# Paged keys by an indirect DMA over 128 partitions, transposed in 32x32 blocks on VectorE, in a hybrid decoder step

## What is computed

```python
cache_k, cache_v (DEPTH, N_PHYS_PAGES, PAGE_SIZE, N_HEADS, HEAD_DIM)   # 1, 160, 128, 8, 128
page_table       (DEC_BATCH, N_PAGES) int32                            # 8, 16
idx, valid = dsa_select(iq, iw, ik_all, q_pos, topk)                   # best 256 of 2056 keys
k_sel, v_sel = rows idx of the paged cache, or of the 8 new keys
logits = einsum('bthd,btkhd->bthk', q, k_sel) * ATT_SCALE + rel_bias[rel_bucket(q_pos - idx)]
out = einsum('bthk,btkhd->bthd', softmax(where(valid, logits, -inf)), v_sel)
```

## Time and profile before

| | |
|---|---|
| median of 3 runs | 1597.6 us (1593.25 to 1598.45) |
| profiled execution | 1593.25 us, span 1593.2 us |
| mean granted TensorE clock | 0.957 |
| key stages, first to last matmul | 464.6 to 582, 705.9 to 812 us |
| value stages | 595.7 to 705.9, 828.4 to 929 us |
| bytes read from HBM | 240.28 MB |

### The profile page before, as it was taken

How to read it: one execution, slowest core, us unless ns; L and a number is a source line. 1 busy time by engine, 2 the same in 40 slices (tenths; PEclk the granted TensorE clock), 3 DMA queues, 4 the chain that set the end, 5 groups by cost and what they waited for, 6 DMA issues and landing times.

```text
span 1593.2 us, 32571 instructions
## 1 busy us (share of the span) xinstructions
PE 1471.7 (92%) x13518; PEld 1334.5 (84%) x13518; DVE 762.0 (48%) x1030; ACT 511.5 (32%) x818; POOL 234.5 (15%) x371
## 2 busy tenths in 40 slices
PE   7999998979979989899998998899799999999995
PEld 4867798957867778797777998799699999999995
DVE  5288699496514540025540135543555555552123
ACT  4243223324323341023341122122344455442121
POOL 3423234154210000000000000321000110000000
PEclk8899999989999999999999999899799999999998
DMA  5415223122159979999869976133322233223221
GB/s 173 149 27 159 65 80 113 57 96 73 49 188 369 332 249 342 383 358 329 310 223 402 363 258 240 34 125 104 113 80 80 80 90 95 83 98 102 79 83 60
DMA packets 179278, 266.58 MB, mean 167 GB/s; under 512 B 20522, under 2 KB 136539, under 8 KB 178043
## 3 DMA queue, kind: packets, MB, share of 16 engines
q1 hardware_dynamic: 167947, 243.95, 44.5%
q0 software_dynamic: 5104, 11.11, 2.1%
q10 hardware_dynamic: 6080, 9.44, 1.6%
HBM read 240.28 MB, written 24.18 MB: 166 GB/s over the span
## 4 chain that ended last, share of the span: by engine, by line
PE 77%; DVE 8%; DMA 5%; ACT 3%; SPq 2%; issue 2%; POOL 2%; ACTq 0%; DVEq 0%
PE PS L987 14%; PE PS L989 13%; PE PS L988 13%; PE PS L1197 8%; PE PS L1210 4%; PE PS L1245 3%; PE PS L1319 3%; PE PS L1318 3%; PE PS L1317 3%; DMA R<-in_cache_v 3%; PE PS L1028 2%; PE PS L1029 2%; PE PS L1030 2%; PE PS L1173 1%; PE PS L1120 1%
## 5 line engine op out<-in xcount | busy, mean ns | idle before, releaser
L987 PE MATMUL PS<-xn_hi,WH 128*128 128x288 f32 (+1 forms) x1424 | 430.7, 302 | 16.0 <-DVE xn_lo L1614 13.2
L988 PE MATMUL PS<-xn_lo,WH 128*128 128x288 f32 (+1 forms) x1424 | 424.7, 298 | 0.0
L989 PE MATMUL PS<-xn_hi,WL 128*128 128x288 f32 (+1 forms) x1424 | 424.6, 298 | 0.0
L987 PEld LDWEIGHTS PS<-xn_hi,WH 128*128 128x128 f32 (+1 forms) x1424 | 271.1, 190 | 33.1 <-issue 22.2
L988 PEld LDWEIGHTS PS<-xn_lo,WH 128*128 128x128 f32 (+1 forms) x1424 | 271.9, 191 | 0.0
L989 PEld LDWEIGHTS PS<-xn_hi,WL 128*128 128x128 f32 (+1 forms) x1424 | 271.6, 191 | 0.0
L582 DVE TENSOR_TENSOR WL<-W,WH 128x2048 fp32r<-128x2048 f32 (+2 forms) x69 | 145.7, 2112 | 241.6 <-ACT WH L1358 241.6
L1358 ACT ACTIVATE WH<-W 128x2048 fp32r<-128x2048 f32 (+2 forms) x81 | 145.1, 1791 | 90.2 <-PE PS L1319 74.9
L1197 PE MATMUL PS<-CST,R 128*128 128x128 f32 x1024 | 142.7, 283 | 9.8 <-DMA R<-in_cache_k 9.5
L1793 DVE COPY RB<-PS 128x512 f32<-128x512 f32 x128 | 88.3, 691 | 115.7 <-PE PS L1197 115.7
L1197 PEld LDWEIGHTS PS<-CST,R 128*128 128x128 f32 x1024 | 112.1, 143 | 35.9 <-issue 25.7
(11 more groups left out here) (257 smaller groups left out, 2423.2 us busy)
## 6 DMA issues: line engine op xcount, KB each, us to landing
R<-in_cache_k SPq DMA_DIRECT2D x128, 512.0 KB, 5.3
R<-in_cache_v SPq DMA_DIRECT2D x128, 512.0 KB, 7.0
W<-in_w_in SPq DMA_DIRECT2D x30, 1024.0 KB, 5.4
W<-in_w_up SPq DMA_DIRECT2D x44, 512.0 KB, 4.6
W<-in_w_down SPq DMA_DIRECT2D x16, 704.0 KB, 4.4
x_scratch<-xT SPq DMA_DIRECT2D x2, 2304.0 KB, 9.0
W<-in_w_branch_a SPq DMA_DIRECT2D x4, 1024.0 KB, 7.9
W<-in_w_branch_b SPq DMA_DIRECT2D x4, 1024.0 KB, 6.1
```

Source lines behind the costliest of these rows:

```text
L987: pe.matmul(out, hi[:, k, cols], x.hi_block(n)[:, tokens], start=first, stop=False)
L988: pe.matmul(out, hi[:, k, cols], x.lo_block(n)[:, tokens], start=False, stop=False)
L989: return pe.matmul(out, lo[:, k, cols], x.hi_block(n)[:, tokens], start=False, stop=last)
```

## The change

Keys are now loaded four pages at a time: one indirect DMA (`load_keys`), issued by GpSimd, takes 128 rows of 16 KB, each of them four successive keys of one page, 32 rows from the page of each of four requests, into 128 partitions. `KROW` holds the row numbers, worked out on GpSimd from the page table (page number x 32 + lane). Two such tiles of 2 MB take the place of the ring's eight pages. VectorE turns a tile in two halves of four heads by 32x32 block transposes into three buffers `KTB`; a block transpose leaves partition 32b+d with number d of 32 of request b's rows. TensorE multiplies these directly: for each head four products over 32 of the 128 dimensions each, with `QB`, in which the queries lie block-diagonally by request; the PE transposes, their PSUM tiles `kp` and the copies to `KTb` go. The keys then stand in the order (key mod 4, key div 4). So mask and bias are read in that order (`by_rest`), and value pages are loaded so that row 4k+r of a page lands in partition 32r+k.

`QB` is cleared by GpSimd and filled by 32 activations on ScalarE. The mask's store and its reload for the first group move from SP's queue to ScalarE's. The tiles `kl` and `o` take one single bank each in the place of a pair. Five side tiles now stand in the key stage of each group (after tiles 2, 5, 8, 11, 14), two in each softmax, one in each of the value stage's first seven requests, two at the start, one at the end. The first eight value pages of a group wait for the transposes of the last two key tiles, and the first two key tiles of the second group for value pages 60 and 64.

```diff
     side = ([('sv', c, r) for c in range(4) for r in range(R)] + [('ga', c) for c in range(8)]
             + [('gb', c) for c in range(8)] + [('su', c) for c in range(8)])
     SIDE_B = [(1, 1), (1, 1), (1, 1), (1, 1), (1, 2), (1, 2), (1, 2), (1, 2)]
-    two, three = {7: 1, 16: 1}, {4: 1, 10: 1, 16: 1}
-    SIDE_V = [two, two, two, three, two, two, three, {4: 1, 10: 1}]
+    SIDE_K = [2, 5, 8, 11, 14]
+    SIDE_V = [{8: 1}, {8: 1}, {8: 1}, {8: 1}, {8: 1}, {8: 1}, {8: 1}, {}]
     side_at, todo = {}, list(side)
 
...
     for G in range(2):
-        put_side(('softmax', G, 0), 1)
+        for kp in SIDE_K:
+            put_side(('K', G, kp), 1)
+        put_side(('softmax', G, 0), 2)
...
-        QZ = R3[:, 4352:6400].rearrange("p (h b c) -> p h b c", h=H, b=8)
+        QB = R3[:, 4352:6400].rearrange("p (g h j c) -> p g h j c", g=2, h=H, j=4)
         kTn = blocks(R3[:, 6400:7424], H)
-        KTb = [blocks(RB[:, 1024 * i:1024 * i + 1024], H) for i in range(2)]
+        KR = [blocks(R1[:, 4096 * i:4096 * i + 4096], 4) for i in range(2)]
+        KTB = [blocks(a, 4) for a in (RB[:, 0:2048], R3[:, 0:2048], R3[:, 2048:4096])]
...
-            G, kind, n = (seq - 8) // 128, (seq - 8) // 64 % 2, (seq - 8) % 64
-            if kind == 0:
-                e.wait_ge(single_filled, single.slots['kp', G, n, 1][0] + 1)
+            G, kind, n = seq // 128, seq // 64 % 2, seq % 64
+            if kind == 0 and n >= 8:
+                e.wait_ge(S_("k_transposed"), 32 * G + 2 * (n // 4 - 1))
+            elif kind == 0:
+                e.wait_ge(S_("v_pages_used"), 64 * G - 4 + 4 * (n // 4))
+            elif n < 8:
+                e.wait_ge(S_("k_transposed"), 32 * G + 30 + 2 * (n // 4))
             else:
-                e.wait_ge(S_("v_pages_used"), 64 * G + n + 1)
+                e.wait_ge(S_("v_pages_used"), 64 * G + n - 7)
...
+        def load_page(e, seq):
+
+            if seq >= 256:
+                return
+            G, kind, n = seq // 128, seq // 64 % 2, seq % 64
+            page_freed(e, seq)
+            v = page_id(e, 4 * G + n // 16, n % 16)
+            e.dma_start(ring[seq % 8], cache_v[0, bass.ds(v, 1)].rearrange("o (k r) h d -> (o r) k (h d)", r=4))\
+                .then_inc(page_in[seq % 8], 16)
+
+        def load_keys(e, G, kp):
+
+            page_freed(e, 128 * G + 4 * kp)
+            e.indirect_dma_start(out=R1[:, 4096 * (kp % 2):4096 * (kp % 2) + 4096], out_offset=None,
+                                 in_=cache_k[0].rearrange("n (k r) h d -> (n k) (r h d)", r=4),
+                                 in_offset=bass.IndirectOffsetOnAxis(ap=KROW[:, 16 * G + kp:16 * G + kp + 1], axis=0))\
+                .then_inc(key_in[kp % 2], 16)
...
             side_loads('start')
-            for seq in range(4):
-                load_page(seq)
-
-            sp.wait_ge(S_("sample_mask"), 1)
-            sp.dma_start(mask_scr, S).then_inc(S_("mask_out"), 16)
-            sp.wait_ge(S_("mask_out"), 16)
-            for j in range(4):
-                sp.dma_start(MG[32 * j:32 * j + 32, :], mask_scr[0:32, :]).then_inc(S_("mask_in0"), 16)
-            for seq in range(4, 8):
-                load_page(seq)
+
             for G in range(2):
-                for n in range(64):
-                    load_page(128 * G + n + 8)
+                for kp in range(NPAGES):
+                    side_loads('K', G, kp)
+                for n in range(8):
+                    load_page(sp, 128 * G + 64 + n)
                 side_loads('softmax', G, 0)
                 side_loads('softmax', G, 1)
                 for b in range(4):
                     for kp in range(NPG):
                         if kp < NPAGES:
-                            load_page(128 * G + 64 + 16 * b + kp + 8)
+                            if 16 * b + kp + 8 < 64:
+                                load_page(sp, 128 * G + 64 + 16 * b + kp + 8)
                         side_loads('V', G, b, kp)
...
+            pool.wait_ge(S_("rows_in"), 64)
+            pool.wait_ge(S_("consts_in"), 16)
+            link(pool.tensor_copy(RB[:, 32:64], PROW[:, :]))
+            link(pool.tensor_scalar(RB[:, 32:64], RB[:, 32:64], 32.0, const('lane')[:, 0:1], ALU.mult, ALU.add))
+            link(pool.tensor_copy(KROW[:, :], RB[:, 32:64]))
...
+            pool.memset(QB, 0.0).then_inc(S_("queries_cleared"), 1)
+            load_keys(pool, 0, 0)
...
-                for n in range(65):
-                    if n < 64:
-                        seq = 128 * G + n
-                        pe.wait_ge(page_in[seq % 8], 16 * (seq // 8 + 1))
-                        for u in range(2):
-                            claim(pe, 'kp', G, n, u)
-                            for i in range(4):
-                                h = 4 * u + i
-                                last = pe.transpose(bank('kp', G, n, u)[:, P * i:P * i + P],
-                                                    ring[seq % 8][:, HD * h:HD * h + HD], ident)
-                            done(last, 'kp', G, n, u)
-                    if (G, n) == (0, 1):
+                for kp in range(NPAGES):
+                    if (G, kp) == (0, 0):
                         pe.wait_ge(S_("sample_queries"), 1)
-                    if n:
-                        kp, bb = (n - 1) // 4, (n - 1) % 4
-                        if bb == 0:
-                            claim(pe, 'kl', G, kp)
-                        for u in range(2):
-                            drained(pe, 'kp', G, n - 1, u)
-                            for j in range(4):
-                                h = 4 * u + j
-                                last = pe.matmul(pbank('kl', G, kp)[32 * j:32 * j + 32, u, 0:P],
-                                                 QZ[:, h, 4 * G + bb, :], KTb[(n - 1) % 2][:, h, :],
-                                                 start=(bb == 0), stop=(bb == 3))
-                        if bb == 3:
+                    claim(pe, 'kl', G, kp)
+                    for u in range(2):
+                        pe.wait_ge(S_("k_transposed"), 32 * G + 2 * kp + u + 1)
+                        keys = KTB[(2 * kp + u) % 3]
+                        for j in range(4):
+                            for c in range(4):
+                                last = pe.matmul(bank('kl', G, kp)[32 * c:32 * c + 32, P * u:P * u + P],
+                                                 QB[:, G, 4 * u + c, j, :],
+                                                 keys[:, :, P * c + 32 * j:P * c + 32 * j + 32],
+                                                 start=(j == 0), stop=(j == 3))
+                        if u == 0:
+                            last.then_inc(S_("k_half_used"), 1)
+                        else:
                             done(last, 'kl', G, kp)
+                    sides('K', G, kp)
...
-                for n in range(64):
-                    filled(dve, 'kp', G, n, 1)
-                    dve.tensor_copy(KTb[n % 2][:, 4:8, :], blocks(bank('kp', G, n, 1), 4))\
-                        .then_inc(drains('kp', G, n, 1), 1)
-                    if n % 4 == 0 and n:
-                        logits(n // 4 - 1)
-                    if n == 48:
+                def transposed(kp):
+
+                    dve.wait_ge(key_in[kp % 2], 16 * (8 * G + kp // 2 + 1))
+                    for u in range(2):
+                        n = 2 * kp + u
+                        if n in (1, 2):
+                            if G == 0:
+                                filled(dve, 'pv', H - 1)
+                            else:
+                                filled(dve, 'o', 0, 3)
+                        if n >= 3:
+                            if n % 2 == 0:
+                                filled(dve, 'kl', G, (n - 3) // 2)
+                            else:
+                                dve.wait_ge(S_("k_half_used"), 16 * G + (n - 3) // 2 + 1)
+                        elif G and n == 0:
+                            filled(dve, 'kl', 0, NPAGES - 1)
+                        dve.transpose(KTB[n % 3], KR[kp % 2][:, :, 512 * u:512 * u + 512])\
+                            .then_inc(S_("k_transposed"), 1)
+
+                for kp in range(NPAGES):
+                    transposed(kp)
+                    if kp >= 2:
+                        logits(kp - 2)
+                    if kp == 13:
                         drained(dve, 'kl', G, 11)
                         dve.tensor_reduce(EARLY, LS[:, :, 0:12 * P], AX_X, ALU.max)
+                    splits('K', G, kp)
...
+def by_rest(a):
+
+    return a.rearrange("p (k r) -> p r k", r=4)
```

92 lines of the change are left out of this document (54 added, 38 removed).

## The result

The changed kernel took **2067.95 us** (median of four runs, 2066.54 to 2069.21). The kernel before, run beside it, took 1595.42 us (median of four, 1592.35 to 1598.45). The ratio is 1.296, with a 95% interval of 1.293 to 1.299: 472 us slower. The prediction was slower, 2004 us, 1960 to 2120. (Medians are those of executions at the usual clock; one of twelve of run 9, 1965 us at a granted clock of 0.64, is left out.)

A forecast was written before the change was run, and what follows sets the result against it. It took TensorE and the DMA engines as both nearly full, with value-page loads on four engines deciding: key rounds plus 336 us per value stage end at 1335 instead of 929.05, + 406 on 1597.6 gives 2004 us, range 1960 to 2120.

The forecast's parts named there:

- The deciding step: Value-page loads: the source's outermost count of 4, not the destination's 128, sets the engines, so four of sixteen work.
- The price of a page: Value stages: a 524288-byte page on four engines takes 5.03 to 5.89 us, taken as 5.12 (409 GB/s).
- The rival of sixteen engines: Value loads: the four don't decide, both stages gain, 1557 us; chance 0.10, with the slow loop 0.04.
- The sum: Whole kernel: last value product at 1335 instead of 929.05, so + 406 us on 1597.6, giving 2004 us.
- From the first keys to the first value page: First key stage: keys issued at 447, transposed 460.4, seven rounds of 13.6 us, tile 14 done at 555.6.
- the mask's way through HBM: First key stage: 8.0 + 5.9 us, moved to ScalarE's queue, lands near 469 before the third tile; costs nothing.
- The first value stage: First group: 336 us of value-page transfers plus 5 for the next group's first key tile, ending at 897.
- The second key stage: Second group: tile 2 transposed near 918, tile 14 six rounds later at 999; 102 us from 897.
- The second value stage: Second group: value-page transfers take 336 us, from 999 to 1335.
- The rivals of a slow key loop: Key stages of 140 us and more; chance 0.14 with four engines, 0.04 with sixteen.
- The ends of the range: Total time: low 1960 with pages at 5.03 and a tile each 5.7 us; high 2120.
- The check list: Value stages: pages land tens of us late, DMA near a quarter, TensorE waits some 500 us; key tiles 6 to 7 us.

The follow-up runs named there:

- run 9: Run 4's kernel (whole-tile key loads) with each key-stage side tile cut into four pieces; 1598.7 us, ratio 1.004.
- Run 1: The kernel before, with only the value-page load changed to a source walked as 4 x 32 x 1024; 2049.7 us, ratio 1.288.
- run 2: The changed kernel with the value-page source walked as 8 x 16 x 1024 in place of 4 x 32 x 1024; 1757.7 us, ratio 1.104.
- run 10: Run 4's natural-order kernel with each value page written as 4 blocks of 32 successive rows; 1600.2 us, ratio 1.005.
- run 4: The changed kernel with keys put back in natural order when VectorE writes the logits, value pages plain 128 x 1024 loads; 1600.3 us, ratio 1.004.
- run 5: The changed kernel with the value-page source walked in 32 outer runs in place of 4; 1597.9 us, ratio 1.004.
- run 6: Run 4's kernel with the ten key-stage side tiles moved into the value stages; 1604.7 us, ratio 1.007.
- run 8: Run 7's half-tile kernel with each key-stage side tile cut into four pieces, one behind each half key tile; 1581.5 us, ratio 0.993.
- run 7: Run 4's kernel with each key tile loaded as two 1 MB halves, each reloaded after its own transpose; 1586.1 us, ratio 0.995.
- run 3: The changed kernel with the value-page source walked in 16 outer runs in place of 4; 1662.4 us, ratio 1.044.
- run 11: Run 4's natural-order kernel with each value page written as 16 blocks of 8 successive rows; 1598.2 us, ratio 1.003.

## Why the prediction was right, and where its sum was short

**The deciding step held.** "I take the 4" was the choice between a row that showed no case and a reading of packet counts. Run 1 isolates it: 28.8 of the 29.6% come with that line alone. The price of a page was taken as 5.12 us and is 5.08. The traces make it four and eight engines for four and eight runs, by 1536 and 1024 packets fewer than on sixteen. Where only value pages move, the DMA share is 0.26 at 103 GB/s with four runs (704 to 712 us) and 0.51 at 206 GB/s with eight (run 2, 656 to 664 us), near a quarter and a half of the sixteen. What counted was the pattern as the instruction carries it: run 10, whose four blocks were joined in the instruction, has the 149563 packets of sixteen engines. The reason given for the 4, that both sides must be cut into the same pieces, was the author's argument, and no trace shows it. Nor does a row of before show that every page takes the same four engines, on which the 336 us of a stage and the 5 us for the next key tile rest; in the changed kernel the share is 0.26 while some four pages are under way (each lands some 22 us after its issue, one each 5.08 us).

**The rival of sixteen engines** (0.10 and 0.04) fell. Its condition was met artificially in runs 4 and 5, and the 1557 us it named were not there: 1600 and 1598. The step that failed in it is the way through the keys to the first value product: it had 581 us, run 4 has 599.7 (keys until 580.5, then a gap of 19.2 us where 15.5 was taken), and from the end of the first values to the first value product of the second group it had 127 us, where run 4 has 142.5.

**The sum was 64 us short: 2004 against 2068.** In trace time, term by term:

- *From the first keys to the first value page*, predicted 555.6, issued at 570.4: 14.8 more. The issues of the key loads (start us, us, what, in brackets GpSimd's wait ahead):

```profile
446.76 1.07 POOL L648 DMA_INDIRECT R<-in_cache_k,KROW  x1 [0.17 <-issue]
...
464.06 1.02 POOL L648 DMA_INDIRECT R<-in_cache_k,KROW  x1 [4.29 <-DVE R L1840]
...
482.62 0.94 POOL L648 DMA_INDIRECT R<-in_cache_k,KROW  x1 [13.22 <-DVE R L1840]
...
497.01 0.94 POOL L648 DMA_INDIRECT R<-in_cache_k,KROW  x1 [6.16 <-DVE RB L1840]
...
511.49 0.94 POOL L648 DMA_INDIRECT R<-in_cache_k,KROW  x1 [6.83 <-DVE R L1840]
...
525.78 0.93 POOL L648 DMA_INDIRECT R<-in_cache_k,KROW  x1 [6.17 <-DVE R L1840]
...
539.49 0.94 POOL L648 DMA_INDIRECT R<-in_cache_k,KROW  x1 [4.14 <-DVE RB L1840]
...
553.71 0.94 POOL L648 DMA_INDIRECT R<-in_cache_k,KROW  x1 [4.28 <-DVE R L1840]
```

  The first of each pair of buffers goes round in 17.3, 18.6, 14.4, 14.5, 14.3, 13.7 and 14.2 us. The step said 13.6. The model was right and its steady part 0.6 us a round short, 7.1 us a tile where the text had 6.8. Most of the error is in the first two rounds. In the first, a weight split stood on VectorE from 457.1 to 459.3, ahead of the transposes. In the second, the load issued at 464.06 landed at 477.84, 13.8 us. In that stretch the engines moved 1.30 MB for ScalarE's queue, most of it the mask, beside 3.13 MB of keys at a DMA share of 1.03, and their packets took 38.4 and 57.0% of the sixteen engines' time: the mask's way through HBM, costed at nothing, has its part in that share. Then VectorE's reduction of 3.35 us stands ahead of tile 14, and its transposes end at 569.7, 16.0 us after the issue. So neither the mask ("nothing") nor VectorE's work ("hidden") was free: what stands between the issue of a tile and the freeing of its buffer lengthens the round. The steady 0.6 us are mostly the flight: the text took 9 us for a tile, and the chain of the second group has 9.44 for one.

- *The first value stage*, 341 predicted, 570.4 to 935.2, 364.8 measured: 24 more. Pages do come each 5.08 us where nothing else passes. Against 64 pages at 5.08 the stage lost 40 us, where the sum allowed 16. The products of the fifth page start here:

```profile
607.84 1.08 PE L1262 MATMUL PS<-R,R 128*32 128x128 f32 x16 [4.43 <-DMA R<-in_cache_v]
```

  That is 37.4 us after the first issue, where five pages at 5.08 are 25.4. The DMA view of 580 to 610 us:

```profile
q1 hardware_dynamic: 553, 2.18, 20.7%
q0 software_dynamic: 192, 1.11, 19.5%
q10 hardware_dynamic: 432, 0.88, 7.8%
...
R<-in_cache_v SPq DMA_DIRECT2D x4, 512.0 KB
SR<-mask_scratch POOLq DMA_DIRECT2D x4, 272.0 KB, 7.5
```

  2.18 MB in 30 us are 73 GB/s, not 103. The mask's reload for the second group (1.1 MB by GpSimd) and three stored side tiles share the engines with the pages. The sum had the stores on its list, but not the reload. Another 11.5 us are lost from 607.84 to 700.65, where sixteen pages take 92.8 us and not 81.3 and two chunks of weights pass, for which the sum had 5 us. The last 43 pages lose 14, about what it allowed.

- *The second key stage*, 102 predicted from the end of the values to the next value page, 117.7 measured: 16 more. Six of them are the rounds, of 14.4 to 15.2 us here. The other 9.7 come at the end, by a wait that the sum did not have. The chain from 1028 to 1080 us, and SP's waits from 1000 to 1060 us:

```profile
1020.72 9.44 DMA R<-in_cache_k,KROW
...
1038.68 4.51 DVE R L1840 x2
...
1051.60 0.37 SPq L666
...
1052.93 0.62 SPq L642
```

```profile
SPq L666 <- PE PS L1014: 87.6, 2, 43.9
```

  Tile 14 is transposed at 1043.2, and the pages might go out. But a chunk of weights (L666) stands ahead of them in SP's queue and waits for the end of TensorE's side tile to get its buffer; it goes out at 1051.60, and the first page behind it. The text had looked at chunks that stand behind pages, not at pages behind a chunk.

- *The second value stage*, 336 predicted, 347.1 measured: 11 more. The first seventeen pages take 100.1 us and not the 86.4 of 5.08 each, with that chunk, another one and the stores beside them; the others come each 5.2.

Together 14.8 + 23.8 + 15.7 + 11.1 = 65 us in trace time (1335 against 1400.0); by medians it is 64, since the kernel before took 1595.4 beside this one where the sum started from 1597.6. All four terms were short; only the 5.12 us taken for 5.08 made up for 3 us a stage.

**The rivals of a slow key loop** (0.14 and 0.04) fell. No run shows key stages of 140 us and more: they are 119.3 and 115.2 us, a tile takes 7.1 us, and run 6 ran the loop at a granted clock of 0.62 to 0.64 in less time (111.7 and 110.1 us). Half of the 64 us by which the sum was short lies in the value stages, outside that loop. The ends of the range were the author's estimates. No run shows the tile each 5.7 us of the low end: whole tiles came each 7.1 us, and run 8, with halves, took 7.0 and 6.1 us a tile over its key stages (111.9 and 97.7 us for 16). The high end of 2120 has a slow loop in it, which no run shows.

**The check list** held: a page lands some 22 us after its issue (the chain has 21.84 us from 678.77), the share is 0.29 to 0.31 at 109 to 112 GB/s, TensorE's wait for value pages is 462 us for "some 500". Only the key tiles follow each other by 7.1 us, more than "6 to 7 us".

**Why the idea does not pay even without the bad load.** Run 4 takes the transposes off TensorE (its busy time falls by 99 us), and wins nothing, because the transfers were nearly full before and the key stage got a new pace setter: two buffers of 2 MB, each 9 to 10 us in flight and 4.5 us under transposition. Runs 7 and 8 against run 9 show that: with halves the same bytes come faster, with whole tiles a smoother TensorE changes nothing. What is left in run 8 beside the transfers is chiefly the two gaps for the softmax, 24.3 and 22.7 us, longer than the 15.5 and 16.4 of before. No run shortened them, so what that would bring is not shown.

## What to carry to other kernels

Look at the outermost count of every transfer whose rows are permuted. On SP's queue a load that took its rows in four or eight interleaved runs ran on four or eight of the sixteen engines (112 and 208 GB/s, against 371); other counts below 16 were not tried. And a change of order is far cheaper in an access pattern of VectorE, where run 4 paid next to nothing for it (431 ns for a read of products instead of 416, from 500 to 556 us). Before taking work off the busiest engine, read what the transfers have left in that stage: here 5 to 8% was all there was, whatever TensorE gave up. And where two buffers go round between a load and its consumer, every microsecond of the round counts (rounds of 14.2 us gave a tile each 7.1); halving the piece helped here, and then the wait moved to another engine. Where many engines share one issuing queue, look too at what stands ahead of the transfer that everything waits for: here a chunk of weights held the second group's pages back by 10 us.

## What the runs showed of the hardware that was not expected

- **Sixteen outer runs are slower than thirty-two** (run 3): with all engines busy (1.04) 279 GB/s against 361. Between 620 and 690 us the 4096-byte packets take 249 ns in the middle, where four, eight and thirty-two runs and natural order have 160 to 162 (the 261 ns of run 11's expectation belong to a stretch 10 us earlier). The bytes, the packet count of the queue (149563) and SP's issue time (0.54 us) are those of thirty-two runs, so none of them makes the difference. The expectation of run 5 laid it on the partitions that an engine writes, and run 5 came out as it said; but which rows and partitions fall to an engine, in the permuted loads or in the plain one, was the author's assumption and no trace shows it. The cause stays open.
- **An issue on SP took longer where the pages went through four engines.** The issuing instruction of a value page, in the value stage of the changed kernel and of run 4 (duration ns min/median/max, first and last start):

```profile
L642 SPq DMA_DIRECT2D R<-in_cache_v x53: 616/3682/12112, 610.3 to 888.1; - x53
```

```profile
L642 SPq DMA_DIRECT2D R<-in_cache_v x48: 332/333/828, 609.9 to 684.1; - x48
```

  0.33 us becomes 3.7, at the worst 12.1 (behind a weight chunk), where sixteen and thirty-two runs have 0.54; whatever is queued behind on SP is issued late by it; a weight chunk issued between pages landed 24.9 us after its issue. That is why "SPq L642" and not the transfer itself heads the chain of the changed kernel.
- **An indirect load of 128 rows cost GpSimd 0.94 us to issue,** whether its rows are 16 KB (run 4) or 8 KB (run 7: 0.94 in the middle, once 3.0). Halving the piece doubles that time, 30 us to 62 us over the kernel, and GpSimd had it to spare.
